# RWKV-7 chunk inverses: identity products left out, blocks turned by VectorE, wide and last merges interleaved, a shorter preparation, groups of four pairs

## The chip, the cores and the metric

The kernel runs on one core of a Trainium2 chip. The metric is the device time of one execution in microseconds (us), as the median of a few runs. The engines are named as in the profile: PE is TensorE's matmul stream, PEld its weight loads, DVE is VectorE, ACT ScalarE, POOL GpSimd and SP SyncE. They run their own instruction streams and meet at semaphores.

## What is computed

Two model blocks on 256 tokens of width 1024. The first has a gated feed-forward net, a mixer of sparse and forgetting attention, a cross attention to a memory and a second feed-forward net. The second block has an RWKV-7 time mix with a feed-forward net, and then a sliding-window attention with another. The change is in the RWKV-7 time mix alone, whose reference is a recurrence over the tokens:

```python
def wkv7(r, w, k, v, a, b):
    def step(S, inp):
        r_t, w_t, k_t, v_t, a_t, b_t = inp
        sa = jnp.einsum('bhvk,bhk->bhv', S, a_t)
        S = S * w_t[:, :, None, :] + sa[..., None] * b_t[:, :, None, :] + v_t[..., None] * k_t[:, :, None, :]
        y = jnp.einsum('bhvk,bhk->bhv', S, r_t)
        return S, y
...
kk = split(k * k_k)
kk = kk / jnp.maximum(jnp.sqrt(jnp.sum(kk * kk, axis=-1, keepdims=True)), 1e-12)
k_mod = k * (1.0 + (a - 1.0) * k_a)
y = wkv7(rh, wh, kh, vh, -kk, kk * ah)
...
y = y + jnp.sum(rh * kh * r_k.astype(f32), axis=-1, keepdims=True) * vh
```

There are 16 heads of 64 channels, kept as 8 pairs of heads, and the tokens are cut into two halves of 128.

## The kernel before

All large matrices come in 1 MB tiles through a ring of four buffers. Each tile is cut into a high part by ACT (line 294) and a rest by DVE (line 304), and PE forms three products of each (lines 344 to 346). The RWKV part stands between two such stretches, and nearly all of it is float32 work on data that is already in the core. It runs in blocks, at whose end all engines meet.

- `rwkv_projections`: PE makes r, k and v from 12 tiles (`rT`, `kT`, `v`), ACT copies each bank out (line 2037 for r and k), and the small "lora" products follow, of which ACT makes `ldT`, `aT` and `gT`.
- `rwkv_prepare`: DVE scales k to `bT`, sums the logarithms of the decays (a scan, line 2094), makes the modified keys `kmT`, the products of the bonus term `rk` (lines 2111 and 2112) and the inverse of the norm (line 2116), while ACT makes the exponentials `ep`, `em` and `before`. PE warms up with `keep_busy` (line 354: products of the identity, whose results nobody reads), sums the squares (line 2162), sums the bonus (line 2169) and spreads the inverse norm over the channels (line 2175). DVE then multiplies everything together (lines 2125 to 2134) into `bT`, `kmT` and `AR`. POOL fills the factor of the scan (lines 2138 and 2140).
- `rwkv_inverses`: a triangular 128x128 matrix is to be inverted for each of 32 units (2 halves of tokens, 16 heads). PE makes the diagonal 32x32 blocks (line 2245) and the whole Gram matrices (2253), and turns `bT` and `kmT` (2259). Meanwhile DVE inverts the 16x16 diagonal blocks of all units at once (`solve_blocks`), and turns the result (lines 2361 and 2362, `t16` and `a16`). PE passes the time with `keep_busy` 40. From then on PE merges blocks in stages, each for two groups `g` of 16 units: `step` (lines 2269 and 2270), `t32` (2278), `narrow` (2288 to 2292), `cross` (2300 to 2305), `late` (2313 and 2314), then `wide` (2319) and `last` (2329) on 64x64 blocks in four groups of 8 units. After each group ACT and DVE copy its banks from `ps` (the PSUM) to the tiles that the next stage reads: DVE on lines 2367 to 2382, ACT on line 2390, both on 2336 and 2341. A float32 product is two matmul instructions and two weight loads.
- `rwkv_halves`: 16 steps of a pipeline, one for a half of the tokens and a pair of heads, in the order that `place(n)` gives: all eight pairs of the first half, then of the second.
- `rwkv_group_norm` and the output product follow, and are not changed.

Nothing schedules this work: each engine's order is the order in which its function writes it.

## Time and profile before

| | us |
|---|---|
| median of 3 runs (lowest to highest) | 1677.97 (1676.77 to 1680.48) |
| the profiled execution, own time | 1681.65 |
| its span in the profile | 1680.3 |
| PE busy in it | 1541.7 (92%) |
| PE weight loads | 1471.3 (88%) |
| DVE busy | 958.1 (57%) |
| ACT busy | 709.5 (42%) |

The profile lists for each instruction its start from the start of the span, its duration and the idle time of its engine before it, with what ended that. An idle time that ended by "issue" is one in which the profile shows no semaphore that the engine waited for. A span of PE is modelled at its end, since matmuls overlap; the starts are exact.

### The profile page before, as it was taken

How to read it: one execution, taken by the hardware profiler on the slowest of the kernel's cores; microseconds unless marked ns; L12 is line 12 of the kernel's file. 1: busy time of each engine (PE TensorE's matmuls, PEld its weight loads, DVE VectorE, ACT ScalarE, POOL GpSimd, SP SyncE). 2: the span in 40 equal slices, each digit the busy share in tenths (PEclk: the TensorE clock that was granted, in tenths of full speed). 3: DMA queues.
4: the chain of work that ended last, by engine and by line, in shares of the span. 5: the costliest groups of instructions: out<-in, count | busy, mean ns of one | idle time of the engine just before them, and what ended most of it. 6: DMA issues, size and time to landing. Idle time of an engine off the chain costs nothing. (4 is left out here: it accounts for less than half of the span.)

```text
span 1680.3 us, 30380 instructions
## 1 busy us (share of the span) xinstructions
PE 1541.7 (92%) x13492; PEld 1471.3 (88%) x13492; DVE 958.1 (57%) x1290; ACT 709.5 (42%) x1078; POOL 7.7 (0%) x11
## 2 busy tenths in 40 slices
PE   8999999998899799999799667987999997799999
PEld 8999998686899799999797366877999996689999
DVE  5665652457764356555564573336665665766555
ACT  5444443344464244444354312223444462454443
POOL 0000000000000000000000010000000000000000
PEclk9999998889999899999799556798999997999999
DMA  6555562420455045555252000003445540145552
GB/s 256 200 191 184 178 217 84 176 101 2 151 178 177 22 176 176 188 188 181 74 178 98 25 2 4 26 1 126 164 174 190 201 153 24 47 142 179 186 200 76
DMA packets 33034, 222.45 MB, mean 132 GB/s; under 512 B 3887, under 2 KB 5167, under 8 KB 6536
## 3 DMA queue, kind: packets, MB, share of 16 engines
q1 hardware_dynamic: 31848, 219.45, 36.7%
q8 instruction: 106, 1.74, 0.4%
q10 hardware_dynamic: 1056, 1.07, 0.2%
q14 instruction: 24, 0.20, 0.0%
HBM read 219.44 MB, written 1.06 MB: 131 GB/s over the span
## 5 line engine op out<-in xcount | busy, mean ns | idle before, releaser
L304 DVE TENSOR_TENSOR tile_lo<-ring,tile_hi 128x1024 fp32r<-128x1024 f32 x396 | 477.5, 1224 | 405.6 <-ACT tile_hi L294 404.9
L294 ACT ACTIVATE tile_hi<-ring 128x1024 fp32r<-128x1024 f32 x396 | 408.7, 1053 | 350.4 <-PE ps L346 328.2
L344 PE MATMUL ps<-hT_hi,tile_hi 128*128 128x256 f32 x1600 | 456.6, 285 | 9.7 <-DVE hidden_lo L753 7.6
L345 PE MATMUL ps<-hT_lo,tile_hi 128*128 128x256 f32 x1600 | 453.3, 283 | 0.0
L346 PE MATMUL ps<-hT_hi,tile_lo 128*128 128x256 f32 x1600 | 453.2, 283 | 0.0
L344 PEld LDWEIGHTS ps<-hT_hi,tile_hi 128*128 128x128 f32 x1600 | 306.9, 192 | 13.5 <-DVE hidden_lo L753 8.0
L345 PEld LDWEIGHTS ps<-hT_lo,tile_hi 128*128 128x128 f32 x1600 | 306.8, 192 | 0.0
L346 PEld LDWEIGHTS ps<-hT_hi,tile_lo 128*128 128x128 f32 x1600 | 306.4, 192 | 0.0
L346 PE MATMUL ps<-hidden_hi,tile_lo 128*128 128x256 f32 x864 | 243.2, 281 | 0.0
L345 PE MATMUL ps<-hidden_lo,tile_hi 128*128 128x256 f32 x864 | 243.0, 281 | 0.0
L344 PE MATMUL ps<-hidden_hi,tile_hi 128*128 128x256 f32 x864 | 243.0, 281 | 0.0
L345 PEld LDWEIGHTS ps<-hidden_lo,tile_hi 128*128 128x128 f32 x864 | 162.7, 188 | 0.0
L346 PEld LDWEIGHTS ps<-hidden_hi,tile_lo 128*128 128x128 f32 x864 | 162.6, 188 | 0.0
L344 PEld LDWEIGHTS ps<-hidden_hi,tile_hi 128*128 128x128 f32 x864 | 162.6, 188 | 0.0
L709 ACT ACTIVATE hidden_hi<-hidden_whole 128x512 fp32r<-128x512 f32 x54 | 34.1, 632 | 115.7 <-DVE hidden_whole L740 66.9
L354 PEld LDWEIGHTS ps<-const_sb 128*128 128x128 f32 x456 | 61.1, 216 | 18.3 <-issue 17.7
L354 PE MATMUL ps<-const_sb 128*128 128x128 f32 x456 | 65.3, 305 | 12.4 <-DMA const_sb<-const 7.1
L998 ACT ACTIVATE scores<-scores,lane_stats 128x256 f32<-128x256 f32 (+1 forms) x88 | 39.4, 449 | 62.6 <-DVE lane_stats L1035 41.5
L753 DVE TENSOR_TENSOR hidden_lo<-hidden_whole,hidden_hi 128x512 fp32r<-128x512 f32 x54 | 37.4, 693 | 40.6 <-ACT hidden_hi L709 20.6
L974 PE MATMUL ps<-const_sb,scores 128*128 128x128 f32 x136 | 22.8, 315 | 25.6 <-ACT weightsT L1017 13.1
L746 DVE TENSOR_TENSOR hidden_whole<-gate,token_scale 128x512 f32<-128x512 f32 x32 | 22.1, 692 | 37.8 <-ACT gate L706 37.8
L344 PE MATMUL ps<-mixed_hi,tile_hi 128*128 128x256 f32 x128 | 37.0, 289 | 6.7 <-DVE mixed_lo L1944 6.7
(462 smaller groups left out, 2406.0 us busy)
## 6 DMA issues: line engine op xcount, KB each, us to landing
ring<-stream SPq DMA_DIRECT2D x204, 1024.0 KB, 4.8
x_sb<-x SPq DMA_DIRECT2D x4, 256.0 KB, 4.0
bias<-f_dram ACTq DMA_DIRECT2D x1, 1024.0 KB, 8.9
squares<-mem SPq DMA_DIRECT2D x1, 1024.0 KB, 4.8
cum<-rows SPq DMA_DIRECT2D x1, 1024.0 KB
out<-x_sb SPq DMA_DIRECT2D x4, 256.0 KB, 2.2
small_sb<-small SPq DMA_DIRECT2D x1, 485.5 KB, 9.3
const_sb<-const SPq DMA_DIRECT2D x1, 417.0 KB, 9.5
```

The source lines that it names most:

```text
L294: act.activation(e.w_hi[:, n % SPLIT, :], e.ring[:, tile % RING, span(n % 2, HALF)], ACT.Copy).then_inc(e.tile_hi.handle, 1)
L304: dve.tensor_tensor(e.w_lo[:, n % SPLIT, :], e.ring[:, CUT[n // 2] % RING, span(n % 2, HALF)], e.w_hi[:, n % SPLIT, :].bitcast(F32), ALU.s ...
L344: pe.matmul(out, left[0], right[0], start=start, stop=False)
L345: pe.matmul(out, left[0], right[1], start=False, stop=False)
L346: return pe.matmul(out, left[1], right[0], start=False, stop=stop)
L354: pe.matmul(e.ps[:, bank, 0:P], ident, ident, start=True, stop=True)
L709: act.activation(slot(hid[0], j), whole[:, j % 2, :], ACT.Copy).then_inc(*hi_ready.one())
L746: link.done(dve.tensor_tensor(halves_of(both), halves_of(tmp[:, j % 2, :]), scale_pairs(e), ALU.mult))
L753: dve.tensor_tensor(slot(hid[1], j), both, slot(hid[0], j).bitcast(F32), ALU.subtract).then_inc(*hidden_ready.one())
L974: tr = pe.transpose(e.ps[:, 4 + at // 512, at % 512:at % 512 + P], s[:, u % DEPTH, lane, kb * P:(kb + 1) * P], const(e, "ident"))
L998: x = act.activation(lanes(step)[:, lane], lanes(step)[:, lane], ACT.Exp, bias=st[:, 0, lane:lane + 1], accum_out=st[:, 1, lane:lane + 1])
```

## The change

In `rwkv_projections`, ACT also writes `bT` (k times `k_k`) from the bank of each k tile, two instructions a tile. In `rwkv_prepare` this product is gone from DVE; the factor exp(-0.5) of the log decays is applied in the exponentials and no longer in a pass of its own on ACT; `r_k` is multiplied into small weights (`rk_sum`, 8 instructions of 128x2) and no longer into `rk`; `before`, the exponential of the previous token's sum, isn't made any more: `ep`, shifted by one token, takes its place. The inverse norm comes before the keys on DVE, PE keeps busy 30 products longer and spreads the norm before it sums the bonus.

In `rwkv_inverses`, PE makes the diagonal blocks of one head of each pair first, so DVE may start on them earlier. POOL clears `step`, and the step's product is no longer accumulated on an identity product: only half of its columns are copied, and the 32x32 inverse is one product per block whose upper right 16x16 part is copied into `diag` beside the 16x16 inverses. Its turned form comes from two DVE transposes (`t32`) and not from PE, so that the stages `t32` and `late` are gone, `narrow` has two products per unit and no longer four, and `cross` three and no longer four. `wide` and `last` are issued alternately, `last` two groups behind. In `rwkv_halves`, the order of the steps is by groups of four pairs: first half, second half, then the other four pairs.

```diff
@@ -2035,6 +2035,10 @@
+                    if n == 1:
+                        for m in range(2):
+                            x = act.activation(w.bT[:, 2 * i + m, :], bank[:, span(m, SEQ)], ACT.Copy,
+                                               scale=small(e, "k_k")[:, 2 * i + m:2 * i + m + 1])
@@ -2077,20 +2082,18 @@
-            dve.tensor_tensor(w.bT[:, :, :], w.kT[:, :, :], over("k_k"), ALU.mult).then_inc(*kk_ready.one())
-
             dve.wait_ge(*restarts.at(1))
-            dve.wait_ge(*logs.at(1))
             link.done(dve.tensor_tensor_scan(all2(cum), all2(before), all2(w.ldT), 0.0, ALU.mult, ALU.add))
...
@@ -2099,39 +2102,41 @@
+            for pair in range(PAIRS):
+                x = dve.tensor_scalar(rk_sum[:, pair, :], head_sum[:, pair, 2 * pair:2 * pair + 2],
+                                      small(e, "r_k")[:, pair:pair + 1], None, ALU.mult)
+            x.then_inc(*weights_ready.one())
+            dve.wait_ge(*sums_done.at(1))
+            dve.wait_ge(*root.at(1))
+            link.done(dve.tensor_scalar(inv[:, 0, :], inv[:, 0, :], 1e-12, None, ALU.max))
+            dve.reciprocal(inv[:, 1, :], inv[:, 0, :]).then_inc(*inv_ready.one())
...
-            link.done(dve.tensor_tensor(rk, w.rT[:, :, :], w.kmT[:, :, :], ALU.mult))
-            dve.tensor_tensor(rk, rk, over("r_k"), ALU.mult).then_inc(*rk_ready.one())
...
-            dve.wait_ge(*cum_ready.at(1))
-            dve.tensor_tensor(all2(before), all2(cum), all2(w.ldT), ALU.subtract).then_inc(*prev_ready.one())
-
-            dve.wait_ge(*exps.at(2))
-            dve.tensor_tensor(all2(w.kmT), all2(w.kmT), all2(em), ALU.mult)
+            dve.tensor_tensor(rk, w.rT[:, :, :], w.kmT[:, :, :], ALU.mult).then_inc(*rk_ready.one())
...
+            dve.scalar_tensor_tensor(out=AR3[:, :, 0, 1:P], in0=chunked_(w.bT)[:, :, 1:P], scalar=-1.0,
+                                     in1=chunked_(ep)[:, :, 0:P - 1], op0=ALU.mult, op1=ALU.mult)
+            dve.wait_ge(*scale_out.at(1))
+            link.done(dve.scalar_tensor_tensor(out=AR3[:, :, 0, 0], in0=chunked_(w.bT)[:, :, 0], scalar=-1.0,
+                                               in1=first.rearrange("p m t -> p (m t)"), op0=ALU.mult, op1=ALU.mult))
+            link.done(dve.tensor_tensor(all2(w.bT), all2(w.bT), all2(w.aT), ALU.mult))
+            dve.tensor_tensor(all2(w.bT), all2(w.bT), all2(em), ALU.mult)
             dve.tensor_tensor(AR3[:, :, 1, :], chunked_(w.rT), chunked_(ep), ALU.mult)
-            dve.wait_ge(*exps.at(3))
-            link.done(dve.scalar_tensor_tensor(out=AR3[:, :, 0, :], in0=chunked_(w.bT), scalar=-1.0, in1=chunked_(before),
-                                               op0=ALU.mult, op1=ALU.mult))
-            link.done(dve.tensor_tensor(all2(w.bT), all2(w.bT), all2(w.aT), ALU.mult))
-            link.done(dve.tensor_tensor(all2(w.bT), all2(w.bT), all2(em), ALU.mult))
+            link.done(dve.tensor_tensor(all2(w.kmT), all2(w.kmT), all2(em), ALU.mult))
@@ -2141,18 +2146,15 @@
-            act.activation(all2(w.ldT), all2(w.ldT), ACT.Copy, scale=-float(np.exp(-0.5))).then_inc(*logs.one())
-            act.wait_ge(*kk_ready.at(1))
             act.activation(sq, w.bT[:, :, :], ACT.Square).then_inc(*squared.one())
...
-            act.activation(all2(ep), all2(cum), ACT.Exp).then_inc(*exps.one())
-            act.activation(all2(em), all2(cum), ACT.Exp, scale=-1.0).then_inc(*exps.one())
+            act.activation(all2(ep), all2(cum), ACT.Exp, scale=-decay).then_inc(*exps.one())
+            act.activation(all2(em), all2(cum), ACT.Exp, scale=decay).then_inc(*exps.one())
             act.wait_ge(*scale_in.at(1))
-            act.activation(w.zscale[:, 3, :, 0], late[:, :, 0], ACT.Exp)
-            act.wait_ge(*prev_ready.at(1))
-            act.activation(all2(before), all2(before), ACT.Exp).then_inc(*exps.one())
+            act.activation(w.zscale[:, 3, :, 0], late[:, :, 0], ACT.Exp, scale=-decay)
+            act.activation(first, mid, ACT.Exp, scale=decay).then_inc(*scale_out.one())
@@ -2162,19 +2164,21 @@
-            pe.wait_ge(*rk_ready.at(1))
...
+            keep_busy(e, pe, 30, 3)
...
+            pe.wait_ge(*weights_ready.at(1))
+            pe.wait_ge(*rk_ready.at(1))
...
+                    mm = pe.matmul(e.ps[:, 1, at:at + 2], rk[:, pair, t * P:(t + 1) * P],
+                                   rk_sum[:, pair, :], start=True, stop=True)
@@ -2205,31 +2209,36 @@
             pool.memset(v.turned[0:BLK, :, BLK:2 * BLK], 0.0).then_inc(*cleared.one())
+            pool.wait_ge(*solved.at(1))
+            pool.memset(step.rearrange("p s n -> p (s n)"), 0.0).then_inc(*emptied.one())
@@ -2238,15 +2247,15 @@
-            for i in range(UNITS // 2):
-                for q in range(QS):
-                    for par in range(2):
+            for par in range(2):
+                for i in range(UNITS // 2):
...
-            mm.then_inc(*diag_done.one())
+                mm.then_inc(*diag_done.one())
@@ -2265,71 +2274,65 @@
-                        out = e.ps[rows(q), 2 * q + g, span(s % 16, BLK)]
-                        pe.matmul(out, ident[rows(q), rows(q)], ident[rows(q), rows(q)], start=True, stop=False)
-                        mm = pe.matmul(out, gu[rows(q), s, :], t16[rows(q), s, :], start=False, stop=True)
+                        mm = pe.matmul(e.ps[rows(q), 2 * q + g, span(s % 16, BLK)], gu[rows(q), s, :], t16[rows(q), s, :],
+                                       start=True, stop=True)
...
-                for s in range(16 * g, 16 * g + 16):
-                    for q in (0, 2):
-                        mm = pe.matmul(e.ps[rows(q), 2 * q + g, span(s % 16, BLK)], a16[rows(q), s, :], step[rows(q), s, :],
...
+                for s in range(16 * g, 16 * g + 16):
+                    for q in range(QS):
+                        mm = pe.matmul(e.ps[rows(q), 2 * q + g, span(s % 16, BLK)], step[rows(q), s, :], diag[rows(q), s, :],
...
+                pe.wait_ge(*t32_placed.at(g + 1))
...
-                    pe.matmul(e.ps[rows(1), g, at], step[rows(1), s, :], a16[rows(1), s, :], start=True, stop=True)
-                    pe.matmul(e.ps[rows(3), 4 + g, at], step[rows(3), s, :], a16[rows(3), s, :], start=True, stop=True)
-                    pe.matmul(e.ps[rows(1), 6 + g, at], v.gram[rows(0), s, rows(1)], v.turned[rows(0), s, 0:BLK],
+                    pe.matmul(e.ps[rows(1), 6 + g, at], v.gram[rows(0), s, rows(1)], t32[rows(0), s, :],
...
-                    mm = pe.matmul(e.ps[rows(3), 2 + g, at], v.gram[rows(2), s, rows(3)], v.turned[rows(2), s, 0:BLK],
...
-                    pe.matmul(e.ps[rows(1), 6 + g, at], a16[rows(1), s, :], step[rows(1), s, :], start=True, stop=True)
-                    pe.matmul(e.ps[rows(1), 4 + g, at], v.full[rows(1), s, rows(1)], v.narrow[rows(1), s, :],
+                    pe.matmul(e.ps[rows(1), 4 + g, at], diag[rows(1), s, :], v.narrow[rows(1), s, :], start=True, stop=True)
+                    pe.matmul(e.ps[rows(2), 2 + g, at], v.narrow[rows(3), s, :], diag[rows(3), s, :], start=True, stop=True)
+                    mm = pe.matmul(e.ps[rows(0), g, at], v.narrow[rows(1), s, :], diag[rows(1), s, :], start=True, stop=True)
-            for g in range(2):
...
-                    pe.matmul(e.ps[rows(2), g, at], step[rows(2), s, :], a16[rows(2), s, :], start=True, stop=True)
-                    mm = pe.matmul(e.ps[rows(0), 2 + g, at], step[rows(0), s, :], a16[rows(0), s, :], start=True, stop=True)
...
             pe.wait_ge(*cleared.at(1))
-            for s in range(UNITS):
-                g, at = s // 8, span(s % 8, 2 * BLK)
-                mm = pe.matmul(e.ps[rows(2, 2), 4 + g, at], v.gram[rows(0, 2), s, rows(2, 2)], v.turned[rows(0, 2), s, :],
...
-            pe.wait_ge(*late_copied_a.at(2))
-            pe.wait_ge(*late_copied_b.at(2))
-            for s in range(UNITS):
-                    pe.wait_ge(*wide_copied[g % 2].at(g // 2 + 1))
-                mm = pe.matmul(e.ps[rows(0, 2), g, at], v.wide[rows(2, 2), s, :], v.full[rows(2, 2), s, rows(2, 2)],
...
+            pe.wait_ge(*t11_placed.at(1))
+            for g in range(6):
+                if g in (0, 2):
+                    pe.wait_ge(*cross_copied_b.at(g + 2))
+                    pe.wait_ge(*cross_copied_a.at(g // 2 + 1))
+                if g >= 2:
+                    pe.wait_ge(*wide_copied[g % 2].at((g - 2) // 2 + 1))
+                    pe.wait_ge(*a32_placed.at(1))
+                for k in range(8):
+                    if g < 4:
+                        first = wide(g, k)
+                    if g >= 2:
+                        second = last(g - 2, k)
+                if g < 4:
+                    first.then_inc(*wide_done.one())
+                if g >= 2:
+                    second.then_inc(*last_done.one())
@@ -2340,6 +2343,12 @@
+        def step_copy(copy, g, q, done):
+            copy(step[rows(q), units(g), low], blocks(2 * q + g, rows(q))[:, :, low]).then_inc(*done.one())
+
+        def diag_copy(copy, g, q, done):
+            copy(diag[upper(q), units(g), high], blocks(2 * q + g, upper(q))[:, :, high]).then_inc(*done.one())
@@ -2348,38 +2357,45 @@
...
-                dve.wait_ge(*t32_done.at(g + 1))
-                copy(v.turned[rows(2), units(g), 0:BLK], blocks(4 + g, 2)).then_inc(*t32_copied_b.one())
-            dve.wait_ge(*cleared.at(1))
+                dve.wait_ge(*a32_done.at(g + 1))
+                for q in (2, 3):
+                    diag_copy(copy, g, q, a32_copied_b)
+                dve.wait_ge(*a32_copied_a.at(2 * g + 2))
+                dve.wait_ge(*a32_copied_b.at(2 * g + 2))
+                dve.transpose(t32[:, units(g), :].rearrange("p s i -> p (s i)"),
+                              diag[:, units(g), :].rearrange("p s i -> p (s i)")).then_inc(*t32_placed.one())
...
+            copy(v.turned[rows(0), :, 0:BLK], t32[rows(0), :, :])
+            copy(v.turned[rows(1), :, BLK:2 * BLK], t32[rows(1), :, :]).then_inc(*t11_placed.one())
@@ -2396,27 +2412,31 @@
...
+            act.wait_ge(*a32_copied_b.at(4))
+            for q in (2, 3):
+                x = copy(v.full[rows(q), :, rows(q)], diag[rows(q), :, :])
+            x.then_inc(*a32_placed.one())
...
@@ -2474,7 +2494,7 @@
-    place = lambda n: (n // PAIRS, n % PAIRS)
+    place = lambda n: (n // GROUP % TT, n // (TT * GROUP) * GROUP + n % GROUP)
```

PE in `rwkv_prepare`, before (`ps` is the PSUM, `AR` holds the squares and `rk`, `const_sb` the constants, which also feed `keep_busy`):

```order
L354 MATMUL ps<-const_sb 128x128 x10
L2162 MATMUL ps<-AR,const_sb 16x256 [waits kk_squared]
L2162 MATMUL ps<-AR,const_sb 16x256 x7
L2169 MATMUL ps<-const_sb,AR 128x2 [waits rk_ready]
L2169 MATMUL ps<-const_sb,AR 128x2 x15
L2175 MATMUL ps<-kk_inverse,const_sb 128x256 [waits kk_inverse_ready]
L2175 MATMUL ps<-kk_inverse,const_sb 128x256 x7
```

The same place in the changed kernel:

```order
L354 MATMUL ps<-const_sb 128x128 x10
L2164 MATMUL ps<-AR,const_sb 16x256 [waits kk_squared]
L2164 MATMUL ps<-AR,const_sb 16x256 x7
L354 MATMUL ps<-const_sb 128x128 x30
L2171 MATMUL ps<-kk_inverse,const_sb 128x256 [waits kk_inverse_ready]
L2171 MATMUL ps<-kk_inverse,const_sb 128x256 x7
L2179 MATMUL ps<-bonus_weights,AR 128x2 [waits rk_ready,bonus_weights_ready]
L2179 MATMUL ps<-bonus_weights,AR 128x2 x15
```

The spread of the inverse norm (line 2175, now 2171) stood behind the bonus, and now stands ahead of it, behind 30 more identity products.

ACT in `rwkv_inverses`, from the copies of the step to the last one, before (`before` holds `step` and `narrow`, `ep` the turned blocks, `al_T` the inverses, `cum` the result of `wide`):

```order
L2390 ACTIVATE ep<-ps 32x16x32 [waits diagonal_t_done] x2
L2390 ACTIVATE before<-ps 32x512 [waits narrow_done,inverse_cleared]
L2390 ACTIVATE al_T<-ps 32x16x32
L2390 ACTIVATE before<-ps 32x512 [waits narrow_done]
L2390 ACTIVATE al_T<-ps 32x16x32
L2390 ACTIVATE ep<-ps 32x16x32 [waits cross_done]
L2390 ACTIVATE al_T<-ps 32x16x32
L2390 ACTIVATE ep<-ps 32x16x32 [waits cross_done]
L2390 ACTIVATE al_T<-ps 32x16x32
L2390 ACTIVATE al_T<-ps 32x16x32 [waits late_done] x2
L2390 ACTIVATE cum<-ps 64x512 [waits wide_done] x2
```

DVE at the same place in the changed kernel, from its copies of the 32x32 inverses (`diagonal_plain` is `diag`, `diagonal_upper` now holds `t32`):

```order
L2351 COPY diagonal_plain<-ps 16x16x16 [waits diagonal_done,diagonal_x_placed]
L2351 COPY diagonal_plain<-ps 16x16x16
L2388 STREAM_TRANSPOSE diagonal_upper<-diagonal_plain 128x512 [waits diagonal_copied_b,diagonal_copied_a]
L2351 COPY diagonal_plain<-ps 16x16x16 [waits diagonal_done]
L2351 COPY diagonal_plain<-ps 16x16x16
L2388 STREAM_TRANSPOSE diagonal_upper<-diagonal_plain 128x512 [waits diagonal_copied_b,diagonal_copied_a]
L2392 COPY before<-ps 32x512 [waits narrow_done] x2
L2393 COPY ep<-diagonal_upper 32x32x32
L2394 COPY ep<-diagonal_upper 32x32x32
L2397 COPY ep<-ps 32x16x32 [waits cross_done]
L2398 COPY al_T<-ps 32x16x32
```

The turned blocks (`ep`) were results of PE that had to be copied from the PSUM on the way to `narrow`; now DVE transposes them from `diag`, between `a32` and `narrow`, and copies the two that `wide` needs later.

PE at the third group of `wide` in the changed kernel (line 2310 is `wide`, 2315 is `last`):

```order
L2310 MATMUL ps<-ep,rk_T 64x64 [waits wide_copied_act,late_copied_a,cross_copied_a,cross_copied_b]
L2315 MATMUL ps<-al_T,cum 64x64
L2310 MATMUL ps<-ep,rk_T 64x64
L2315 MATMUL ps<-al_T,cum 64x64
L2310 MATMUL ps<-ep,rk_T 64x64
L2315 MATMUL ps<-al_T,cum 64x64
```

Before, all 32 products of `wide` stood ahead of the 32 of `last`; now two of the six groups hold both, alternately.

## Rows read from the trace of the kernel before

**Rows 1.** The page: PE's granted clock in 40 slices of the span, in tenths.
```profile
PEclk9999998889999899999799556798999997999999
```
**Rows 2.** Windows: length, busy us (count) of PE, PEld, DVE, ACT, POOL; clock, DMA share, GB/s.
```profile
944.30:988.30 44.00, 22.48 (x84) 17.84 (x84) 37.28 (x28) 12.48 (x9) 1.94 (x3) 0.58 0.00 0
988.30:1012.00 23.70, 21.05 (x418) 20.35 (x418) 18.61 (x39) 5.45 (x12) 4.38 (x2) 0.74 0.01 3
1012.00:1048.00 36.00, 24.55 (x1281) 23.36 (x1280) 11.50 (x16) 8.60 (x15) 0.00 (x0) 0.58 0.02 4
1048.00:1062.50 14.50, 13.58 (x132) 13.36 (x128) 3.43 (x5) 2.96 (x5) 0.00 (x0) 0.50 0.01 2
1062.50:1072.00 9.50, 9.37 (x45) 7.70 (x46) 5.54 (x5) 0.83 (x3) 1.04 (x2) 0.50 0.30 110
1072.00:1122.00 50.00, 49.53 (x395) 45.00 (x395) 14.18 (x14) 17.16 (x60) 0.00 (x0) 1.00 0.00 1
...
1020.00:1024.00 4.00, 1.97 (x128) 1.83 (x128) 0.00 (x0) 0.00 (x0) 0.00 (x0) 0.50 0.02 4
```
**Rows 3.** Timeline of DVE in the preparation: start, us, what, [idle before it].
```profile
946.57 4.42 DVE L2094 TENSOR_TENSOR_SCAN cum<-before,al_T 128x2048 f32<-128x2048 f32 x1
...
963.86 1.74 DVE L2116 RECIPROCAL kk_inverse<-kk_inverse 16x256 f32<-16x256 f32 x1
...
972.71 0.69 DVE L2125 TENSOR_TENSOR spare<-ps,spare 128x512 f32<-128x512 f32 x1 [2.77 <-PE ps L2175]
...
985.51 2.29 DVE L2134 TENSOR_TENSOR spare<-spare,squares 128x2048 f32<-128x2048 f32 x1
```
**Rows 4.** Timeline of POOL at the start of the preparation.
```profile
946.18 0.13 POOL L2140 MEMSET before<- 128x16 f32 x1
```
**Rows 5.** Timeline of PE in the preparation.
```profile
944.36 4.61 PE L354 MATMUL ps<-const_sb 128*128 128x128 f32 x20 [4.62 <-PEq L1914]
948.90 3.84 PE L2162 MATMUL ps<-AR,const_sb 128*16 128x256 f32 x16
963.69 6.99 PE L2169 MATMUL ps<-const_sb,AR 128*128 128x2 f32 x32 [10.96 <-DVE AR L2112]
970.61 7.19 PE L2175 MATMUL ps<-kk_inverse,const_sb 16*128 16x256 f32 x16
```
**Rows 6.** Windows of 1 us, columns as in Rows 2: the granted clock where it falls.
```profile
925.00:926.00 1.00, 1.00 (x4) 0.42 (x3) 0.00 (x0) 1.00 (x3) 0.00 (x0) 0.73 0.00 0
...
956.00:957.00 1.00, 0.00 (x0) 0.00 (x0) 0.96 (x2) 1.00 (x2) 0.00 (x0) 0.59 0.00 0
```
**Rows 7.** Timeline of ACT: around the last k tile, and a 128x256 one.
```profile
877.92 0.60 ACT L2037 ACTIVATE rk_T<-ps 128x512 f32<-128x512 f32 x1 [1.76 <-PE ps L346]
878.41 1.05 ACT L294 ACTIVATE tile_hi<-ring 128x1024 fp32r<-128x1024 f32 x1
...
915.74 0.38 ACT L2046 ACTIVATE lora_hidden<-ps 128x256 f32<-128x256 f32 x1 [3.28 <-PE ps L1992]
```
**Rows 8.** Timeline of PE where the inverses turn to the merges.
```profile
1002.96 9.10 PE L354 MATMUL ps<-const_sb 128*128 128x128 f32 x80
```
**Rows 9.** Timeline of DVE at the same place.
```profile
1009.46 1.98 DVE L2361 STREAM_TRANSPOSE cum<-cum 128x1024 f32<-128x1024 f32 x1
```
**Rows 10.** Timeline of the weight loads: each row resumes after a stall.
```profile
1016.42 0.10 PEld L2270 LDWEIGHTS ps<-cum,diagonal_upper 32*32 32x32 f32 x1 [2.13 <-issue]
...
1020.42 0.12 PEld L2270 LDWEIGHTS ps<-cum,diagonal_upper 32*32 32x32 f32 x1 [2.63 <-issue]
...
1043.50 0.12 PEld L2301 LDWEIGHTS ps<-al_T,before 32*32 32x32 f32 x1 [0.77 <-issue]
```
**Rows 11.** Groups of PE in the merges, by form: busy us, mean ns, idle before.
```profile
L2303 PE MATMUL ps<-before,al_T 32*32 32x32 f32 x64 | 7.1, 237 | 0.0
L2319 PE MATMUL ps<-ep,rk_T 64*64 64x64 f32 x64 | 7.1, 312 | 0.0
...
L2313 PE MATMUL ps<-diagonal_plain,before 32*32 32x32 f32 x64 | 3.9, 236 | 0.1
```

171 lines of the change are left out of this document (79 added, 92 removed).

## The prediction

> **What bounds the kernel now.** I read PE's granted clock over the whole span first, then windows cut at the stages of the RWKV part, then the timelines of each engine in them. Over most of the span PE works on weight tiles at its high clock; the dent in the middle of the clock row is the RWKV part [rows 1], and only that part is changed. It runs in blocks, so its time is a sum of stages, and in each the reader is to ask who is late. In `rwkv_prepare`, 44.0 us, DVE is busy for 37.3 us and PE for half: DVE's chain is the bound [rows 2]. In the first 23.7 us of `rwkv_inverses` PE is busy 21.05 us and DVE 18.6 [rows 2]. From 1012 to 1048, the merges from `step` to `late`, no engine is: PE 24.55 of 36.0 us, DVE 11.5, ACT 8.6 [rows 2]. The timeline of the weight loads says why: PE stalls with "issue" named, no semaphore, and resumes at 1016.42, 1020.42 and so on to 1043.50; there are seven such intervals, 27.1 us, so 3.87 us each [rows 10]. Between two resumptions stand 128 matmul instructions, as in the window from 1020 to 1024, and their 128 weight loads [rows 2]. So this stretch is paced by how many instructions PE has to be given: 1281 in 36 us. The same spacing appears whether the work is 4 small blocks wide or 2. From 1048 on `wide` and `last` fill PE (13.6 of 14.5 us), and `rwkv_halves` fills it too (49.5 of 50.0 us after the clock has risen) [rows 2].
>
> **The change, part by part.** All sums are made against the profiled execution, 1681.65 us of its own, 3.7 us above the median of the runs, 1677.97; I take the gain found in it off the median.
>
> Projections: ACT gets 8 instructions of 128x256 more, 0.38 us each by the nearest row, 0.76 us a tile [rows 7]. They delay ACT's next high part of a weight tile, and behind it DVE's rest of it. ACT is idle for 1.76 us before each bank it copies, and the high part behind it, 1.05 us, is for a tile half that PE reaches two halves later [rows 7]. I cost it at nothing; if that cover were gone it would be 4 x 0.76 = 3.0 us.
>
> Preparation, 44 us, by DVE's chain. The product to `bT` that stood before the scan is gone, but the scan needs POOL's fill as well, which ends at 946.18 + 0.13 = 946.31 [rows 4]; it started at 946.57 [rows 3]. So of a 2.3 us pass only 0.2 us are gained: scan at 946.4, and what follows it to 953.6 as before. Then 8 instructions of 128x2, between 0.1 us (no work in them) and 0.38 us (the 128x256 of rows 7); I take 0.15, together 1.2, so 954.8. The maximum and the reciprocal, 2.0 us, end at 956.8: before, the reciprocal started at 963.86 [rows 3]. PE has the sums ready at 952.74 in both kernels [rows 5]. Three passes of about 2.3 us [rows 3] make `kmT` and `rk`, to 963.7, and the masks, 0.6, to 964.3. Meanwhile PE runs 60 more instructions of `keep_busy`: at the high clock 9.10/80 = 0.114 us each [rows 8], 6.8 us, from 952.74 to 959.6. This delays the spread of the norm beyond 956.8, but it costs nothing as DVE comes for it at 964.3 only: at half of 7.19 us, since that row ran at the low clock [rows 5], it ends at 963.2. The four waits of 2.77 and three times 1.0 us before DVE's products with it [rows 3] go away; they take 2.5 us, to 966.8. What is late next is the bonus on PE, now behind the spread: 32 instructions, 6.99 us at the low clock [rows 5], from 963.8 to 970.8, or at the high clock to 967.3. DVE's copy of the bonus stands ahead of five passes, all of which queue behind that wait. They are 2.3 us each, 11.5 with 0.3 for the copy and the small first column. So the preparation's last pass ends at 979.0 or 982.5, before at 985.51 + 2.29 = 987.8 [rows 3]: a gain of 8.8 or 5.3 us. Which, depends on the clock. It fell at 956.2 when PE had been idle since 952.74, and at 925.5 amid continuous work of 32-row and 128-row products [rows 5, 6]; the products of 2 columns and of 16 rows, 14 us of them without a gap, never raised it (the stage's mean of 0.58 is 7 us at the high clock, and those ended at 956.2) [rows 2, 5]. So I expect it to fall during the bonus, and take 6.5.
>
> Inverses, first part. DVE may take the diagonal blocks of the first heads while PE makes the second ones, some 1.2 us earlier. But `keep_busy` 40 ends at 1012.06 [rows 8], while the turned inverses were ready at 1009.46 + 1.98 = 1011.44 [rows 9]. PE sets this, and the gain is nothing, up to 1.0 us if the clock rises earlier there. POOL's fill of `step` starts when the solve ends and is 1024 elements wide, under a microsecond in the same 2 us in which DVE transposes. I take 0.
>
> Merges. `step` 512 to 256 instructions, `t32` 128 and `late` 128 to none, one stage `a32` of 256, `narrow` 256 to 128, `cross` 256 to 192: 1280 to 832. At the pace of the stretch, 36.0/1281 = 28.1 ns an instruction [rows 2], 448 fewer are worth 12.6 us. I take this if nothing else is late instead. The candidates: the chain from `a32` to `narrow` has a 16x256 copy on two engines and a transposition of 128x512, which I price at half of 1.98 us [rows 9], so with its copies some 2 us for the second group. By 3.87 us a stretch of 128, PE is given the second half of `narrow` about when it is placed, so up to 1 us; DVE's two 32x1024 copies for `wide`, about 1.1 us each by elements against 0.69 for 512 [rows 3], stand ahead of its copies of `cross`, another 1 us at most. I take 1 us for both: 11.6.
>
> `wide` and `last`: 8 groups, each 16 instructions of 7.1/64 = 0.11 us, 1.75 us [rows 11]. In the change they are 6 groups, if the two kinds run side by side. They use different quarters of the array. The evidence: two kinds of 32x32 products in `late` took 3.9 us for 64 of each [rows 11], so 128 in some 3.9 us, while the same form in `cross`, where two of four share a place, took 7.1 us for 64 [rows 11]: products at different places overlap. Two groups less are 3.5 us, of which I keep 3.4. Together the inverses gain 15.0, between 11 (nothing of the side by side, both waits in full) and 19 (the waits hidden, the clock up).
>
> `rwkv_halves`: the same 16 steps in another order. PE is the bound and the waits of ACT and DVE lie inside its time [rows 2]. The second half of a pair needs that pair's state. It was made 8 steps earlier and will be made 4 steps earlier, with two steps of the pipeline between its copy and its use, at 50 us for some 14 steps 3.5 us each. Nothing is won or lost. The first 9.5 us run at the low clock [rows 2]; where the rise falls may differ by some us, each worth half.
>
> The sum: 6.5 + 15.0 = 21.5 us, so 1656.5 from the median (1660.2 for a profile like the one of before).
>
> **A rule weighed.** The stalls of [rows 10] are the term on which most rests. The Trainium skill, "Runtime: NRT & Kernel Launch", section on instruction fetch mechanics, says that a program is fetched in blocks of 256 instructions and that crossing a boundary is "mostly hidden". The block size fits 128 matmuls with 128 weight loads between resumptions; the hiding doesn't, at 0.8 to 2.6 us a stall. If the page were right in that, the stalls would have another cause and would stay: that is the first rival.
>
> **The rivals.** (1) The stalls don't go with the number of instructions. Then they keep their sum, 36.0 - 24.55 = 11.5 us [rows 2], and only PE's busy time shrinks, from 24.5 to some 14.5 (the identity products and `late` at 15 to 30 ns an instruction): a gain of 10 in place of 12.6, less the 1: 1659. For it: they are named "issue" and not more; against: their even spacing under different work. (2) `wide` and `last` don't overlap, as alternate instructions wait for each other: 3.4 less, 1660. For it: the trace shows no 64x64 pair. (3) The 30 extra products hold the clock high through the bonus, and the waits in the merges are covered: 2.3 + 1 more, or the clock stays up in `rwkv_inverses` longer, up to 4 more: 1651. For: the clock was high until 956.2. (4) Slower than before: the changed PE work is thinner, and the clock isn't raised in `rwkv_halves`. There all 50 us are PE's [rows 2], and would take twice as long: up to 50 us more, 1706. It decides once 21.5 us of that work run at the low clock beyond the first 9.5. Against: the same stage rose by its own work after 9.5 us. (5) The change doesn't do what it says: of the groups of four pairs I say so already, at 0.
>
> **How the numbers follow.** Forecast 1656.5 (1653 to 1659): 0.55. Rival 1: 0.11. Rival 2: 0.08. Rival 3: 0.20. Rival 4: 0.02. Some mishap at a place that I can't see: 0.04, half of it slower, a quarter no change. A range of 1649 to 1663 holds all but the last two and the tail of each, about 0.85. A measurement of this kernel can tell about 0.2%, 3.4 us, from no change: faster 0.95, same 0.01, slower 0.04.
>
> **What would show it.** In the changed profile: DVE's scan at most 0.3 us earlier after the block's start, the spread complete before DVE asks for it, one wait of DVE for the bonus of 0.5 to 4 us, and the block 37 to 38 us long. In the merges: stalls named "issue" still 3.5 to 4 us apart, but six and not eight; no idle time of PE over 1 us that ends by DVE's transposition. `wide` and `last` in six groups of 1.75 us. `rwkv_halves` within 2 us of 59.5. The forecast is wrong if the merges stretch over more than 41 us from the first product to the last copy (before 50), or if an idle time of PE that ends by a semaphore replaces the stalls.

## The result and the profile of the changed kernel

The changed kernel takes 1650.35 us, median of 4 runs (1645.29 to 1654.47). The kernel before, on the same chip, took 1679.22 us (4 runs, 1676.77 to 1681.14). The ratio is 0.9837, with a 95% interval of 0.9806 to 0.9869. This is 28.9 us less where 21.5 were forecast. The wide range of the prediction, 1649 to 1663, holds the median; the narrow one around its own value of 1656.5, 1653 to 1659, does not, and the value named for rival 3, 1651, lies nearer. The profiled run took 1645.29 us, with a span of 1644.0 us.

The clock row of the page, to compare with [rows 1]: the dent is narrower and less deep.

```profile
PEclk9999998899999899999899766989999997999999
```

The windows by stage, with the columns of [rows 2]. The preparation is 934.8 to 973.2; the first part of `rwkv_inverses` goes to 995.5, the merges up to `cross` to 1019.1, `wide` and `last` to 1029.2; then `rwkv_halves` runs to 1089.2. The column behind the engines is the granted clock: 0.50 and 1.00 are TensorE's two levels, 1.2 and 2.4 GHz.

```profile
934.80:973.20 38.40, 26.15 (x144) 22.40 (x145) 31.34 (x34) 8.76 (x8) 1.94 (x3) 0.68 0.00 0
...
973.20:981.00 7.80, 6.39 (x280) 6.19 (x282) 4.80 (x7) 0.51 (x2) 4.35 (x2) 0.50 0.02 5
981.00:982.00 1.00, 1.00 (x14) 1.00 (x12) 0.97 (x2) 0.36 (x1) 0.00 (x0) 0.50 0.00 0
982.00:995.50 13.50, 12.82 (x130) 12.52 (x129) 12.46 (x32) 4.58 (x10) 0.95 (x1) 0.99 0.01 1
995.50:1019.10 23.60, 14.00 (x832) 13.20 (x832) 10.57 (x17) 6.86 (x13) 0.00 (x0) 0.58 0.02 4
1019.10:1029.20 10.10, 9.09 (x135) 8.91 (x128) 4.13 (x6) 4.95 (x7) 0.01 (x1) 0.63 0.01 3
1029.20:1033.20 4.00, 3.97 (x22) 3.42 (x24) 1.92 (x2) 0.28 (x1) 1.03 (x2) 0.59 0.72 260
1033.20:1089.20 56.00, 53.68 (x429) 48.43 (x425) 17.73 (x17) 18.00 (x63) 0.00 (x0) 1.00 0.00 1
```

Cut in the same way, the two profiled executions compare as follows (us). "Rest" is everything from the group norm on.

| | before | after | difference | forecast |
|---|---|---|---|---|
| ahead of the preparation | 944.3 | 934.8 | -9.5 | 0 |
| preparation | 44.0 | 38.4 | -5.6 | -6.5 |
| inverses, first part | 23.7 | 22.3 | -1.4 | 0 |
| merges, `step` to `cross` | 36.0 | 23.6 | -12.4 | -11.6 |
| `wide` and `last` | 14.5 | 10.1 | -4.4 | -3.4 |
| halves | 61.5 | 60.0 | -1.5 | 0 |
| rest | 556.2 | 554.8 | -1.4 | 0 |

From the preparation to the group norm the two profiles lie 25.4 us apart (179.8 against 154.4), and 26.3 with the repeat of the changed kernel (153.5). This is what the change is worth. The 9.5 us ahead of it are not its work: they go with the clock in a part that has the same code in both kernels but for ACT's eight small copies. This is the window from 300 to 600 us of the changed kernel:

```profile
300.00:600.00 300.00, 271.27 (x2200) 248.73 (x2200) 170.16 (x291) 135.89 (x256) 0.00 (x0) 0.97 0.34 124
```

and this the same window of the kernel before, at 0.92, with 80 products fewer in the same time:

```profile
300.00:600.00 300.00, 271.27 (x2120) 248.87 (x2119) 166.71 (x288) 132.82 (x253) 0.00 (x0) 0.92 0.33 120
```

In the profiles of all the kernels that follow, the preparation starts between 938.5 and 950.3 us, in no order that goes with their edits. So I compare the stages and hold the totals beside them. The stages scatter too, but less: the changed kernel, run again later, has a median of 1649.47 us and the same 38.4 and 60.0 us for preparation and halves, but 55.1 us for the inverses and not 56.0, so 153.5 for the stretch. Five profiles have the changed kernel's own code in the inverses (these two, the old order of pairs, and the two edits of the bonus, all below): 56.0, 55.1, 55.3, 55.5 and 55.4 us. The profile shown here is the longest of them, so a difference below 1 us in this stage tells nothing, and what is measured against its 56.0 can be up to 0.9 us too small.

DVE in the preparation, the rows that answer to [rows 3]:

```profile
936.79 4.42 DVE L2097 TENSOR_TENSOR_SCAN cum<-before,al_T 128x2048 f32<-128x2048 f32 x1 [2.30 <-POOL before L2145]
...
944.03 1.13 DVE L2106 TENSOR_SCALAR bonus_weights<-const_sb,small_sb 128x2 f32<-128x2 f32 x8
...
945.38 1.74 DVE L2112 RECIPROCAL kk_inverse<-kk_inverse 16x256 f32<-16x256 f32 x1
...
954.41 2.47 DVE L2126 TENSOR_TENSOR spare<-ps,spare 128x512 f32<-128x512 f32 x4
...
961.16 0.19 DVE L2130 COPY bonus<-ps 128x32 f32<-128x32 f32 x1 [4.27 <-PE ps L2179]
...
970.40 2.28 DVE L2139 TENSOR_TENSOR spare<-spare,squares 128x2048 f32<-128x2048 f32 x1
```

The four products with the spread norm (line 2126) stand in one row without a wait; the one wait left is that for the bonus, 4.27 us. PE in the same stretch, answering to [rows 5]:

```profile
938.62 3.63 PE L2164 MATMUL ps<-AR,const_sb 128*16 128x256 f32 x16
942.18 6.96 PE L354 MATMUL ps<-const_sb 128*128 128x128 f32 x60
949.07 4.93 PE L2171 MATMUL ps<-kk_inverse,const_sb 16*128 16x256 f32 x16
954.07 6.96 PE L2179 MATMUL ps<-bonus_weights,AR 128*128 128x2 f32 x32
```

The bonus takes 6.96 us, the low clock's time of [rows 5]. Windows of 1 us, as in [rows 6], show where the clock fell, in the middle of the spread; the mean of 0.71 in the first puts the fall at 951.4:

```profile
951.00:952.00 1.00, 1.00 (x5) 0.85 (x4) 0.96 (x2) 0.00 (x0) 0.00 (x0) 0.71 0.00 0
952.00:953.00 1.00, 1.00 (x4) 0.72 (x4) 1.00 (x1) 0.00 (x0) 0.00 (x0) 0.50 0.00 0
```

This profile is the exception. In the nine others with this preparation and its 30 products the clock fell 18.5 to 19.1 us after the block's start, where it is 16.7 here, and the spread took 3.7 to 4.0 us. This row is from the kernel with the bonus off DVE's way, below:

```profile
957.43 3.80 PE L2171 MATMUL ps<-kk_inverse,const_sb 16*128 16x256 f32 x16
```

It makes no difference to the stage: in all ten the bonus starts 19.3 us after the block's start, at the low clock, and ends at 26.25.

The stalls of the weight loads, as in [rows 10]:

```profile
999.63 1.20 PEld L2277 LDWEIGHTS ps<-cum,diagonal_upper 32*32 32x32 f32 x83 [2.58 <-issue]
1002.96 1.79 PEld L2286 LDWEIGHTS ps<-diagonal_plain,before 32*32 32x32 f32 x127 [1.54 <-issue]
1006.84 1.16 PEld L2286 LDWEIGHTS ps<-diagonal_plain,before 32*32 32x32 f32 x80 [2.09 <-issue]
1010.88 0.12 PEld L2293 LDWEIGHTS ps<-diagonal_upper,rk_T 32*32 32x32 f32 x1 [1.83 <-issue]
...
1014.62 0.12 PEld L2305 LDWEIGHTS ps<-diagonal_plain,before 32*32 32x32 f32 x1 [0.76 <-issue]
...
1018.57 0.12 PEld L2303 LDWEIGHTS ps<-before,diagonal_plain 32*32 32x32 f32 x1 [1.58 <-issue]
```

From 999.63 to 1018.57 there are five intervals in 18.94 us, 3.79 us each. The pace of before is still there; it is only needed less often: six stalls, where before had eight. No wait of DVE or ACT has taken its place.

The transfers in this stretch fit it. The DMA view of the kernel before, from 1010 to 1045 us, has one queue at work, whose kind is "instruction":

```profile
q8 instruction: 9, 0.15, 1.7%
```

Nine packets in 35 us are one in 3.9 us, and the stalls stand 3.87 us apart. The changed kernel has six such packets from 995.5 to 1019.1, and six stalls. So PE most likely waits for the next block of its program; that it is this transfer and nothing beside it that each stall waits for is inferred from the count.

### The profile page after: what moved, and what is told of

Read it like the earlier page. It is cut to its first block and busy times, and to the rows that moved or that the text cites. A ratio compares the mean times of both kernels' runs of the same rounds, so it can differ in the third digit from the quotient of the medians.

```text
span 1644.0 us, 29625 instructions
## 1 busy us (share of the span) xinstructions
PE 1515.5 (92%) x13104; PEld 1448.2 (88%) x13104; DVE 951.0 (58%) x1298; ACT 708.8 (43%) x1085; POOL 8.6 (1%) x12
## 5 line engine op out<-in xcount | busy, mean ns | idle before, releaser
L354 PEld LDWEIGHTS ps<-const_sb 128*128 128x128 f32 x516 | 67.0, 211 | 18.3 <-issue 17.6
L354 PE MATMUL ps<-const_sb 128*128 128x128 f32 x516 | 71.1, 299 | 12.4 <-DMA const_sb<-const 7.1
L998 ACT ACTIVATE scores<-scores,lane_stats 128x256 f32<-128x256 f32 (+1 forms) x88 | 39.4, 448 | 59.3 <-DVE lane_stats L1035 39.5
L974 PE MATMUL ps<-const_sb,scores 128*128 128x128 f32 x136 | 23.6, 322 | 26.3 <-ACT weightsT L1017 13.8
L974 PEld LDWEIGHTS ps<-const_sb,scores 128*128 128x128 f32 x136 | 18.6, 167 | 29.2 <-issue 16.1
L746 DVE TENSOR_TENSOR hidden_whole<-gate,token_scale 128x512 f32<-128x512 f32 x32 | 22.1, 692 | 37.8 <-ACT gate L706 37.8
```

Of the source, the lines that this page charges most:

```text
L354: pe.matmul(e.ps[:, bank, 0:P], ident, ident, start=True, stop=True)
L746: link.done(dve.tensor_tensor(halves_of(both), halves_of(tmp[:, j % 2, :]), scale_pairs(e), ALU.mult))
L974: tr = pe.transpose(e.ps[:, 4 + at // 512, at % 512:at % 512 + P], s[:, u % DEPTH, lane, kb * P:(kb + 1) * P], const(e, "ident"))
L998: x = act.activation(lanes(step)[:, lane], lanes(step)[:, lane], ACT.Exp, bias=st[:, 0, lane:lane + 1], accum_out=st[:, 1, lane:lane + 1])
```

## The experiments

The edits are shown against the changed kernel, except for the two that do one part alone.

**The identity products put back.** Ahead of each product of `step` stands an identity product again, at the same place of the PSUM. The real product then overwrites it, so the result is as before; only PE's list is longer, by 128 products, which are 256 matmul instructions and 256 loads.

```diff
+                        pe.matmul(e.ps[rows(q), 2 * q + g, span(s % 16, BLK)], ident[rows(q), rows(q)], ident[rows(q), rows(q)],
+                                  start=True, stop=True)
```

> The changed kernel with the 128 identity products (256 matmul instructions, 256 weight loads) put back in the step, each as a product of its own that the real one overwrites. Theory (the merges are paced by the number of PE instructions, 28.1 ns each in the stretch of before): the time from the step's first product to the last copy of cross grows by 256 x 28.1 = 7.2 us, from 23.9 to about 31, in two more stalls named issue. Rival (only the products' own time counts; 128 instructions of this form took 1.97 us in the window 1020 to 1024 of before): 2.5 to 3.9 us more, with as many stalls as now.

The inverses took 62.8 us, 6.8 more than in the changed kernel (56.0), every other stage the same within 0.7. The weight loads stall eight times between the start of `step` and `wide`, and six times in the changed kernel: the two more stalls of the theory. The median was 1661.46 us, ratio 0.9891 (0.987 to 0.9911).

**The same number of products, one column wide.** These are overwritten too.

```diff
+                        pe.matmul(e.ps[rows(q), 2 * q + g, s % 16 * BLK:s % 16 * BLK + 1], ident[rows(q), rows(q)],
+                                  ident[rows(q), q * BLK:q * BLK + 1], start=True, stop=True)
```

> As the run before, but the 128 extra products move one column and not 32, so they have 1/32 of the work and the same number of instructions (256 and 256 weight loads). Theory (number of instructions): again about 7.2 us more than the changed kernel, the same as with the full ones within 1 us. Rival (the work of the products): under 1.5 us more. This run and the one before together tell number from work.

62.9 us, so 6.9 more; median 1658.90 us, ratio 0.9891 (0.9865 to 0.9917). A product of one column costs this stretch as much as one of 32. The group of them in the by-form view of PE, from the kernel with full products:

```profile
L2277 PE MATMUL ps<-const_sb 32*32 32x32 f32 x256 | 7.0, 224 | 1.3 <-DVE cum L2375 1.3
```

and from the one with thin ones (busy us, mean ns, idle before):

```profile
L2277 PE MATMUL ps<-const_sb 32*32 32x1 f32 x256 | 6.4, 179 | 0.0
```

In the latter there are eight stalls as well, 3.47 to 4.01 us apart. Four of them:

```profile
1004.05 0.10 PEld L2279 LDWEIGHTS ps<-cum,diagonal_upper 32*32 32x32 f32 x1 [1.86 <-issue]
1007.78 0.12 PEld L2279 LDWEIGHTS ps<-cum,diagonal_upper 32*32 32x32 f32 x1 [2.38 <-issue]
...
1015.66 1.79 PEld L2288 LDWEIGHTS ps<-diagonal_plain,before 32*32 32x32 f32 x127 [1.98 <-issue]
1019.54 1.15 PEld L2288 LDWEIGHTS ps<-diagonal_plain,before 32*32 32x32 f32 x80 [2.09 <-issue]
```

So it is the number of instructions that costs, not their work: 6.8 us over 256 matmul instructions are 27 ns each, and 30 against the repeat's 55.1 us, where the prediction had 28.1. A fixed time that every product takes on the engine, whatever its width, would give the same totals; it wouldn't give two more stalls, in which PE stands idle.

**The preparation alone**, in the kernel before: the changed `rwkv_prepare` and ACT's copies in the projections, with the old inverses and halves.

> The kernel before with the projections and the preparation of the change alone. In the changed kernel's profile the preparation took 38.4 us from its first keep-busy product to the first product of the inverses (44.0 before). Theory: the same 5.5 us here, and nothing in the other stages but where the clock rises: 1673 to 1674 from 1679.2. Rival (ACT's extra copies delay the projections): the k and v tiles take over 5.76 us each, and the gain is under 4 us.

The preparation took 38.4 us, the inverses 74.3 as before. The median of 10 runs is 1672.17 us against 1679.76 (13 runs), ratio 0.996 (0.9941 to 0.9979): 6.7 us by 0.4%, 6.4 by the stages (5.6 in the preparation, 0.8 in the halves). ACT's copies cost nothing. The timeline of ACT in the changed kernel shows why (in this kernel the tiles stand 5.76 us apart too):

```profile
863.25 0.60 ACT L2037 ACTIVATE rk_T<-ps 128x512 f32<-128x512 f32 x1 [1.76 <-PE ps L346]
863.74 0.83 ACT L2040 ACTIVATE spare<-ps,small_sb 128x256 f32<-128x256 f32 x2
...
869.01 0.60 ACT L2037 ACTIVATE rk_T<-ps 128x512 f32<-128x512 f32 x1 [1.76 <-PE ps L346]
```

The first and the last row are one tile, 5.76 us, apart. ACT's idle time ahead of each is the 1.76 us of [rows 7], although the two copies (0.83 us together) now stand between them.

**The inverses alone**, in the kernel before, with its own preparation.

> The kernel before with the new inverses alone. Theory: the stage shrinks from 74.3 us to 56 to 58, so the time is 1661 to 1663 from 1679.2, and with the preparation alone (5.5) this leaves 1 to 5 us of the measured 28.9 to chance or to the other parts. Rival (the inverses gain less when the preparation's 60 extra instructions don't shift where the stalls fall): 60 to 62 us for the stage.

44.0 us for the preparation and 55.7 for the inverses, 18.6 less than before; median 1656.94 us, ratio 0.9864 (0.983 to 0.9897). From the preparation to the group norm it gained 20.9 us, the preparation alone 6.4. Both together are 27.2, where the change has 25.4 (26.3 by its repeat): the two parts add up but for 1 to 2 us. Most of that lies in `rwkv_halves`, which took 59.2 us here and 60.8 with the preparation alone, against 61.5 before and 60.0 with both. Here the clock is high from before the stage's start; there it rises 5 us into it.

The two kernels also tell where the first part of the inverses gained. `step` began 23.8 us after the block's start in the kernel before, 23.6 with the preparation alone and 24.1 with the inverses alone: neither gained there. With the preparation alone the clock rose 7.7 us after the block's start and not 12.3, but then PE waited 2.5 us for DVE's turned inverses. With the inverses alone DVE was in time, but the clock rose at 12.4 and PE's `keep_busy` ended last.

**The old order of the pairs**, which undoes the groups of four.

```diff
-    place = lambda n: (n // GROUP % TT, n // (TT * GROUP) * GROUP + n % GROUP)
+    place = lambda n: (n // PAIRS, n % PAIRS)
```

> The changed kernel with the order of before in rwkv_halves (eight pairs of the first half, then eight of the second). The stage from POOL's fill of the states to DVE's first sum of the group norm took 61.5 us before, 60.0 in the changed kernel, 59.2 to 59.3 in three runs with new inverses. Theory (the order is worth nothing, the difference is where the clock rises): 59 to 61.5 us. Rival (the groups of four win something): 61.5 or more with a clock that rises no later than 5 us after the start of the stage.

The halves took 60.0 us, as with the groups, and the clock fell and rose at the same places of the stage; the median of 2 runs was 1647.92 us, ratio 0.9817 (0.9789 to 0.9846). The order of the pairs is worth nothing.

**`wide`, then `last`**: the six groups made eight again, with the signals that this needs.

```diff
-            for g in range(6):
+            for g in range(4):
...
-                    if g < 4:
-                        first = wide(g, k)
-                    if g >= 2:
-                        second = last(g - 2, k)
...
+                    first = wide(g, k)
+                first.then_inc(*wide_done.one())
+            pe.wait_ge(*a32_placed.at(1))
+            for g in range(4):
+                pe.wait_ge(*wide_copied[g % 2].at(g // 2 + 1))
+                for k in range(8):
+                    second = last(g, k)
+                second.then_inc(*last_done.one())
```

> The changed kernel with all of wide ahead of all of last, as before. Theory (products at different places of the array overlap when issued alternately; forecast 3.4 us): the inverses take 56.0 + 3.4 = 59.4 us if the clock stays low through last, or about 58 if it rises after 6.8 us of wide as it did at the end of the changed kernel. Rival (alternate instructions don't overlap, the gain there came from the risen clock alone): 56.0 within 0.7 us.

The inverses took 60.3 us, 4.3 more (4.5 counted from the first product of `wide` to the stage's end, 14.55 against 10.05 us; the other four profiles with the inverses' code unchanged have 9.7 to 10.1); median 1658.12 us, ratio 0.9878 (0.9849 to 0.9907). The by-form view of PE in this kernel, once `last` stands alone:

```profile
L2310 PE MATMUL ps<-ep,rk_T 64*64 64x64 f32 x64 | 7.1, 312 | 0.0
L2315 PE MATMUL ps<-al_T,cum 64*64 64x64 f32 x64 | 7.1, 312 | 0.0
```

and in the changed kernel:

```profile
L2310 PE MATMUL ps<-ep,rk_T 64*64 64x64 f32 x64 | 7.1, 312 | 0.0
L2315 PE MATMUL ps<-al_T,cum 64*64 64x64 f32 x64 | 5.8, 274 | 0.0
```

In the latter the two rows add up to 12.9 us in a stretch of 10.1: two of the six groups hold both kinds at once. `last` also has a lower mean there, 274 ns, since the clock rises at about 1026, before the stage ends; I take this for the 1 us over the 3.4 of the forecast.

**Without the 30 extra identity products** ahead of the spread.

```diff
-            keep_busy(e, pe, 30, 3)
```

> The changed kernel without the 30 extra identity products of the preparation. In the changed profile the clock fell at 951.7, 2.6 us after these products, so that they shielded half of the spread (4.93 us) and nothing of the bonus (6.96 us, the low clock's figure). Theory (they are worth nothing): the spread starts at once when the inverse norm is ready, 5 us after the sums, takes up to 7.2 us and ends about when DVE comes for it; DVE's wait for the bonus stays 4.3 us within 1, the preparation 38.4 us within 1. Rival (they hold the clock for the spread, which DVE then waits for): DVE waits 1 us four times again and the preparation takes 40 us or more.

The preparation took 38.6 us (38.4), the inverses 54.7; median 1649.29 us, ratio 0.9826 (0.9797 to 0.9854). PE in this kernel:

```profile
951.60 7.19 PE L2170 MATMUL ps<-kk_inverse,const_sb 16*128 16x256 f32 x16 [3.88 <-DVE kk_inverse L2112]
958.72 6.99 PE L2178 MATMUL ps<-bonus_weights,AR 128*128 128x2 f32 x32
```

Without them the clock falls sooner and the spread takes 7.19 rather than 4.93 us (3.7 to 4.0 in the other profiles), but it also starts as soon as the inverse norm is there. The bonus ends 0.3 us later, and DVE waits 4.53 us rather than 4.27. The extra products hold the clock and also hold PE: they give nothing.

This run tells one thing more. It takes 60 matmul instructions out of PE's list well ahead of the inverses, whose own list is unchanged. If the stalls belonged to certain places of the code, they would stay at the same products. PE's first row in the inverses, up to its first stall there, in the changed kernel and in this one:

```profile
973.20 2.86 PE L2254 MATMUL ps<-AR,spare 64*32 64x32 f32 x202 [12.18 <-PEq L2088]
977.89 1.94 PE L2253 MATMUL ps<-AR,spare 64*32 64x32 f32 x134 [12.18 <-PEq L2088]
```

The first stall comes behind 202 instructions in the one and behind 134 in the other, 68 earlier. If there is a stall every 128 instructions, 60 fewer ahead put each stall 60 later, and the one before it comes into the stage, 128 - 60 = 68 ahead of the old place: this fits to the instruction. The stalls in the merges are 60 instructions later too, within one. So one fewer (five and not six) falls between the start of `step` and that of `wide`, which took 21.4 us where the changed kernel has 23.6 and its repeat 23.0; but `step` began 23.3 us after the block's start and not 22.1 to 22.7.

**One signal for the diagonal blocks**, so that DVE can't take the first heads' blocks early.

```diff
-            for par in range(2):
-                for i in range(UNITS // 2):
-                    for q in range(QS):
+            for i in range(UNITS // 2):
+                for q in range(QS):
+                    for par in range(2):
...
-                mm.then_inc(*diag_done.one())
+            mm.then_inc(*diag_done.one(2))
```

> The changed kernel with the diagonal blocks in the order of before (both heads of a pair alternately) and one signal at their end. Forecast: nothing, as keep-busy products held PE until after the turned inverses were ready. But in the changed profile PE had finished them and waited for the turned inverses, 22.3 us after the start of the stage (23.7 before). If that is so (theory now): the turned inverses are ready 0.9 to 1.3 us later and the stage takes 56.9 to 57.3 us. The forecast's own view: 56.0 within 0.4.

The inverses took 55.6 us, within the 55.1 to 56.0 of the profiles with two signals, and not the 56.9 to 57.3 of my theory. DVE was indeed later: it began to turn the inverses back 21.1 us after the block's start rather than 20.3, and PE waited for it, as the timeline of PE shows.

```profile
1008.55 1.67 PE L2277 MATMUL ps<-cum,diagonal_upper 32*32 32x32 f32 x170 [2.39 <-DVE cum L2373]
```

`step` began 23.2 us after the block's start; in the five profiles with the changed code it began at 22.1 to 22.7. So up to 1.1 us of the first part do hang on this signal, as the theory said. Whether they reach the end can't be told: `wide` began at 46.1 us here and at 45.1 to 46.0 in the five, and the stage's scatter is as large as the effect. That a wait ahead of the merges gives the supply of instructions time to catch up would fit, but it isn't shown. The median of 2 runs, 1660.28 us, lies 10 us above that of the changed kernel, and it isn't this edit: the preparation begins at 947.0 us in its profile, and from there to the group norm there are 153.1 us (154.4).

**The bonus off DVE's way.** `rk` gets another buffer, and the copy of the bonus stands behind the five passes in place of ahead of them.

```diff
-    rk = AR2[:, 2048:4096].rearrange("p (m n) -> p m n", m=KC)
+    rk = before[:, :, :]
...
-            dve.wait_ge(*bonus_done.at(1))
-            dve.tensor_copy(w.bonus[:, :, :].rearrange("p t h -> p (t h)"), e.ps[:, 1, 0:TT * RH])
...
+            dve.wait_ge(*bonus_done.at(1))
+            link.done(dve.tensor_copy(w.bonus[:, :, :].rearrange("p t h -> p (t h)"), e.ps[:, 1, 0:TT * RH]))
```

> The changed kernel with the bonus products kept in the tile of the scan's factors, which is free by then, and with DVE's copy of the bonus moved behind its last pass, so DVE no longer waits for PE's bonus sums (4.27 us). Theory (that wait ends last): the preparation takes 38.4 - 4.3 = 34.1 us, all else is unchanged. Rival (another wait takes its place, such as that for the spread, which ends at 954.0 in the changed profile, 0.4 us before DVE came for it): over 35 us.

The preparation took 34.2 us, 4.2 less: the whole wait. From its timeline of DVE:

```profile
973.44 2.29 DVE L2137 TENSOR_TENSOR spare<-spare,squares 128x2048 f32<-128x2048 f32 x1
975.64 0.19 DVE L2139 COPY bonus<-ps 128x32 f32<-128x32 f32 x1
```

The copy comes last and waits for nothing. From there to the group norm the stages are as in the changed kernel (55.5 and 60.0 us). The median of 2 runs was 1646.22 us, ratio 0.9801 (0.9746 to 0.9856).

**The bonus passes spread** over four steps of `rwkv_halves`. This is aimed at a wait which the profile of the changed kernel shows and that of before doesn't. DVE there:

```profile
1034.80 2.28 DVE L2643 TENSOR_TENSOR ep<-v_rwkv,bonus 128x2048 f32<-128x2048 f32 x1
1037.12 2.29 DVE L2644 TENSOR_TENSOR ep<-ep,cum 128x2048 f32<-128x2048 f32 x1
1039.33 1.81 DVE L2650 TENSOR_TENSOR rk_T<-ps,gram_keep 128x768 int32<-128x768 int32 x2
```

and PE, which waits for the last of these rows:

```profile
1040.33 0.71 PE L2565 MATMUL ps<-v_rwkv,rk_T 128*128 128x128 f32 x4 [1.23 <-DVE rk_T L2650]
```

In the kernel before the same two passes stand at 1069.21 to 1073.82, the first of them wholly where PE still ran at the low clock (until 1072), and PE had no wait for DVE in the stage:

```profile
1069.21 2.28 DVE L2623 TENSOR_TENSOR ep<-v_rwkv,bonus 128x2048 f32<-128x2048 f32 x1
```

The edit:

```diff
-                if n == 3:
+                if n in (6, 8, 10, 12):
...
+                    t = n % 4 // 2
+                    bonus = w.bonus[:, t, :].unsqueeze(2).to_broadcast([P, RH, HD])
+                    shift = flat(w.cum)[:, D:2 * D]
+                    given = flat(w.ep)[:, span(t, D)]
```

> The changed kernel with DVE's two full-width passes for the bonus in rwkv_halves, both ahead of step 3, cut into four half passes ahead of steps 6, 8, 10 and 12. In the changed profile PE waited there 1.4 us for DVE at 1040.33, where before it was still at the low clock and didn't. Theory (the earlier rise of the clock turned DVE's 4.6 us into a wait): halves 60.0 to about 58.5 us. Rival (it was hidden behind the pipeline's other waits): 60.0 within 0.5.

The halves took 58.7 us, 1.3 less, with nearly the clock of the changed kernel, and PE has no wait for DVE left. DVE's first part is short enough to lie inside PE's step:

```profile
1053.06 1.22 DVE L2645 TENSOR_TENSOR ep<-v_rwkv,bonus 128x1024 f32<-128x1024 f32 x1
```

The total (2 runs, 1653.62 us, ratio 0.9845, 0.979 to 0.99) doesn't show it: its preparation starts at 945.1 us.

**All three** edits that cost nothing: the bonus off DVE's way, its passes spread, and the 30 identity products gone.

> Both edits of the two runs before and no 30 extra keep-busy products. Theory: preparation 34.1 to 34.4, inverses 54.7 as in the run without the extra products, halves 58.5: 147.5 us from the start of the preparation to the group norm, 6 to 7 us less than the changed kernel (154.4), so a median of some 1644 if the changed kernel's is 1650 again. Rival (the parts don't add up, since an earlier start of the inverses finds the clock low for longer): under 4 us.

34.2 us, 55.4, 57.6; from the preparation to the group norm 147.1 us, 6.4 less than the changed kernel's repeat. The halves are 1.1 us shorter than with the passes spread alone: the clock doesn't fall at their start here. The median of 6 runs is 1646.06 us (1638.92 to 1648.71), ratio 0.9787 (0.975 to 0.9824), against 1649.47 us and 0.9828 (0.9788 to 0.9868) of the changed kernel's repeat, which follows.

**The changed kernel once more.**

> The changed kernel once more, beside the three others. In nine profiles so far the stretch from the start of the preparation to the group norm took 179.8 us before and 153 to 154.4 us with the change, while everything ahead of it took between 934.8 and 950.3 us whatever the kernel. Theory (the change is worth some 25.4 us, and the rest of the measured 28.9 is chance ahead of the RWKV part): again 153.5 to 155 us in the stretch, and a median between 1648 and 1656. Rival (the change makes the part ahead of it faster too): 938 us or less ahead of the preparation again.

The stretch took 153.5 us, the median is 1649.47 us, and the preparation starts at 938.7 us, so by these signs the theory holds, though the first and the last are near the edge of what was named. Compared with it, the kernel with all three edits shows 6.4 us less in the stages, 3.4 in the medians, and the two intervals overlap. By the stages it is the faster kernel; the totals alone don't prove it.

## Why the prediction was right, point by point

**What bounds the kernel**: right. The count of instructions sets the pace of the merges (the two kernels with 256 more matmul instructions: 6.8 and 6.9 us where 256 x 28.1 ns = 7.2 were due, with two stalls more each). This also settles the rule weighed ahead: the Trainium skill, "Runtime: NRT & Kernel Launch", section on instruction fetch mechanics, has the crossing of a block boundary mostly hidden; here each costs 0.4 to 2.6 us, and work that computes nothing costs as much as work that does. The prediction's lower figure of 0.8 left out a small stall of 0.4 us at 1027.73 in the kernel before. That the stalls go by 128 products with their loads is shown by the kernel without the 30 products, whose stalls moved by 60. With this, rival 1 is ruled out.

**Preparation**: 5.6 where 6.5 was taken, and 5.3 to 8.8 were the bounds. The scan begins 1.98 us after PE's first row of the block, before 2.21: 0.23 gained, forecast 0.2. The bonus weights took 1.13 us (1.2). The spread was complete at 954.0, and DVE came for it at 954.41. The step that failed was the place of the clock's fall. I let it fall during the bonus; it fell ahead of the bonus in every profile with this preparation, by 0.2 to 0.8 us in nine of the ten with the 30 products and within the spread, at 951.4, in the one shown (the expectations of later runs say 951.7). So the bonus ran at the low clock throughout, 6.96 us, and DVE waited 4.27 us, just over the 0.5 to 4 named. The lower bound of the sum, 5.3 with the bonus wholly at the low clock, was the right value, and the 6.5 was 0.9 us too much.

**Inverses, first part**: 1.4 gained where I had 0, and "up to 1.0 if the clock rises earlier". It rose about 9 us after the block's start, before about 12. With that, the 80 products of `keep_busy` ended ahead of DVE, and not behind it: PE's first row of `step` waits 0.69 us for DVE's transposition. The bound changed hands, as the forecast's condition said, for a little more than its price. The prediction had the earlier start of DVE worth nothing since PE ended last. The runs show that it takes both: an earlier rise of the clock alone (the preparation alone) or the two signals alone (the inverses alone) gained 0.2 us or nothing. Why the clock rises earlier isn't settled: it rose 7.6 to 11.9 us after the block's start in the twelve profiles with the new preparation and 12.3 to 12.4 in the two with the old one. In the repeat PE waited 1.11 us for that transposition, more than the 1 us that the prediction allowed in the merges.

**Merges**: 12.4 (13.0 in the repeat) where 12.6 less 1 were forecast. The pace was right; the two waits of 0.5 us each that I took off did not come. This is from prices of DVE that were too high, in the timeline of DVE in the inverses:

```profile
1009.29 0.71 DVE L2388 STREAM_TRANSPOSE diagonal_upper<-diagonal_plain 128x512 f32<-128x512 f32 x1
...
1014.20 0.68 DVE L2393 COPY ep<-diagonal_upper 32x1024 f32<-32x1024 f32 x1
```

The transposition of 128x512 took 0.71 us (I had half of 1.98) and the copy of 32x1024 0.68 us (I had 1.1, by elements from a copy out of the PSUM). There are six stalls, as forecast, and from the first product of `step` to the last copy there are 33.4 us, where more than 41 would have refuted the forecast.

**`wide` and `last`**: the overlap is real, which rival 2 denied: 4.5 us by the kernel that takes it away, of which 3.4 were forecast for two groups less. The rest I put down to the higher clock at its end; no run separates it.

**Halves**: within 0.5 us of the 59.5 named, and the groups of four are worth nothing, as said. Behind the 1.5 us gained stand two things that I hadn't seen and that partly cancel: the low clock at the start lasts 4 us rather than 9.5, which by an estimate (5.5 us at half the pace) gives 2.7 us, and DVE's two passes of 2.3 us then meet PE at the high clock, which takes 1.23 us back.

**The rest of the gain.** By its own steps the forecast had 21.5 us; the stages gave 25.4, the inverses 3.2 of the 3.9 more. By term: the preparation gave 0.9 less than forecast, the merges 0.8 and `wide` with `last` 1.0 more, and two terms put at nothing, the first part of the inverses and the halves, gave 1.4 and 1.5. The further 3.5 us between this and the medians are 1.4 in "rest" and scatter of the part ahead. That scatter is as large as the whole miss, so how near the median came to the forecast is in part chance; the stages are what bears the mechanism out. Rival 3 had a part of the difference right (waits covered, clock up earlier in the inverses) and was wrong in its first half: the 30 extra products did not hold the clock through the bonus, and the kernel without them is as fast. That the median lies next to its 1651 is no sign for it. Rival 4 didn't come about.

## What to carry to other kernels

Where PE stalls with "issue" at even distances, count its instructions and not its work: each matmul instruction with its load cost 27 to 30 ns here, even where it was one column wide. When a chain is made shorter, look again at what stood in its shade (here a copy behind a wait of 4.27 us, and two passes of 2.3 us that had been hidden by a low clock); moving both took another 5.5 us out of their stages. Compare by stages whose ends can be found in both traces, since the part ahead, whose code is the same, took 934.8 to 950.3 us in twelve profiles; the granted clock from 300 to 600 us was 0.97 in the shortest and 0.90 in the longest. And take the same kernel twice before a difference under 1 us is read from a stage.

## What the runs showed of the hardware

- Thin products cost this stretch as much as full ones: 256 matmul instructions more of 32x1 made it 6.9 us longer, 256 of 32x32 made it 6.8.
- In the merges PE stalls once per 128 matmul instructions with their 128 loads, for 0.4 to 2.6 us. With 60 instructions fewer ahead, every stall moved by 60.
- A transposition of 128x512 by DVE between buffers without gaps took 0.71 us, that of 128x1024 in the same stage 1.88 to 2.12, so more than twice as much for twice the elements; whether the layout or the size does it, no run shows. A copy of 32x1024 within the SBUF took 0.68 us, as long as one of 32x512 out of the PSUM (0.68 to 0.70).
- The bonus, 32 products of 2 columns with 128 rows, ran at the low clock for 6.96 us, and in the profile shown the clock fell amid products with 16 rows, though PE was busy without a gap in both. In the nine others with this preparation and its 30 products it fell in the last 0.7 us of them.
- The clock rose for some 4 us at the end of the inverses, fell at about 1030 as `rwkv_halves` began, and rose again at 1033.3. Why it fell there is open; in the kernel with the old order of pairs it fell in the same place. In five of the experiments (both with extra products, one signal, the inverses alone, all three edits) it rose 2 to 4 us ahead of the halves and stayed up; the halves then took 59.2 to 59.3 us, against 60.0 (57.6 with all three edits).
